# A hybrid retention and HGRN2 trunk on eight cores: two loads moved behind other weights, the sample tile moved to the end, and a new model of the DMA queues in the planner

## The reference: what is computed

```
h = RMSNorm(x) * g_pre
u = h @ W_in                       # 1024 x 4096, eight segments of 512 columns:
                                   # rq rk rv rg hq hf hi hg  (segments 0 to 7)
rq, rk = rotary(rq), rotary(rk)
f  = lb + (1 - lb) * sigmoid(hf);  hk = 1 - f;  hq = silu(hq)
o_r, S_ret  = retention(rq, rk, rv, decay per head)     # recurrent over chunks
o_h, S_hgrn = hgrn2(hq, hk, hi, log f)                  # recurrent over chunks
o  = concat(silu(rg) * head_norm(o_r), silu(hg) * head_norm(o_h))
y  = o @ W_out                                           # 1024 x 1024
out = x + RMSNorm(y) * g_post
```

## Time and profile before

| | us |
|---|---|
| median of 3 executions | 387.5 |
| lowest and highest | 386.18, 388.3 |
| the profiled execution | 388.32 |
| its span on core 7, first to last instruction | 386.8 |
| spans of the eight cores | 381.1 to 386.8 |
| TensorE busy on core 7 | 358.8 (93% of the span) |
| VectorE busy | 255.6 (66%) |
| GpSimd busy | 205.5 (53%) |
| ScalarE busy | 180.9 (47%) |

### The profile page before, as it was taken

How to read it: one execution, slowest core, us unless ns; L and a number is a source line. 1 busy time by engine, 2 the same in 40 slices (tenths; PEclk the granted TensorE clock), 3 DMA queues, 4 the chain that set the end, 5 groups by cost and what they waited for, 6 DMA issues and landing times.

```text
span 386.8 us, 8100 instructions; the slowest of 8 cores (381.1 to 386.8 us)
## 1 busy us (share of the span) xinstructions
PE 358.8 (93%) x2339; PEld 188.1 (49%) x2339; DVE 255.6 (66%) x554; ACT 180.9 (47%) x563; POOL 205.5 (53%) x277
## 2 busy tenths in 40 slices
PE   8599799998988989997999999999999999999982
PEld 8554354455544444453545454545455554554541
DVE  0316565827889998969395949386849467486364
ACT  2431245557767546471636253446262533646341
POOL 8525541545775785774283645375837436347130
PEclk9989899999999999998999999999999999999988
DMA  7999999996488476964537335432233443233217
GB/s 177 204 177 165 202 163 168 178 242 150 87 219 173 157 169 146 231 160 102 153 67 190 88 121 73 164 71 64 55 125 72 133 107 97 110 56 79 101 22 225
DMA packets 64700, 52.62 MB, mean 136 GB/s; under 512 B 45840, under 2 KB 53040, under 8 KB 64656
## 3 DMA queue, kind: packets, MB, share of 16 engines
q1 hardware_dynamic: 59344, 41.61, 42.4%
q0 software_dynamic: 5312, 10.49, 17.7%
HBM read 41.73 MB, written 10.09 MB: 134 GB/s over the span
## 4 chain that ended last, share of the span: by engine, by line
PE 78%; DVE 6%; DMA 5%; issue 3%; POOL 3%; ACT 2%; SPq 1%; DVEq 0%; ACTq 0%; POOLq 0%; another core or an unknown queue 0%
PE bank L671 42%; PE bank L947 14%; PE bank L654 12%; DMA xr<-xp 4%; PE bank L867 2%; PE bank L835 2%; DVE xbf L619 2%; PE bank L872 2%; PE bank L884 2%; POOL QTh L731 1%; DVE fG L713 1%; DVE fR L725 1%; PE bank L934 1%; DMA ogT<-og 1%; SPq L849 1%
## 5 line engine op out<-in xcount | busy, mean ns | idle before, releaser
L671 PE MATMUL bank<-Wi,xT 128*128 128x512 bf16 (+1 forms) x816 | 187.8, 382 | 0.7 <-DVE Sst L889 0.7
L671 PEld LDWEIGHTS bank<-Wi,xT 128*128 128x128 bf16 (+1 forms) x816 | 78.3, 99 | 88.1 <-issue 4.1
L947 PE MATMUL bank<-Wo,ogT 128*128 128x512 bf16 (+1 forms) x272 | 65.1, 391 | 3.6 <-DMA ogT<-og 2.0
L905 DVE SCALAR_TENSOR_TENSOR og<-bank,rsq,gate 128x128 bf16<-128x128 f32 (+1 forms) x136 | 38.6, 343 | 41.2 <-POOL rsq L902 18.3
L654 PE MATMUL bank<-xT,Wi 128*128 128x512 bf16 (+1 forms) x320 | 63.0, 342 | 2.1 <-POOL QTh L731 0.9
L654 PEld LDWEIGHTS bank<-xT,Wi 128*128 128x128 bf16 x320 | 26.9, 98 | 34.2 <-issue 6.9
L947 PEld LDWEIGHTS bank<-Wo,ogT 128*128 128x128 bf16 (+1 forms) x272 | 26.5, 100 | 34.7 <-issue 7.4
L824 POOL TENSOR_TENSOR Sst<-Sst,decS 128x512 f32<-128x512 f32 x30 | 32.9, 1105 | 16.5 <-DVE Sst L889 8.7
L895 ACT ACTIVATE og<-bank 128x128 bf16<-128x128 f32 (+1 forms) x136 | 35.4, 291 | 9.7 <-PE bank L867 6.2
L902 POOL TENSOR_TENSOR rsq<-ssq,mhalf 128x4 f32<-128x4 f32 (+1 forms) x34 | 35.4, 1042 | 5.2 <-POOL ssq L899 0.4
L828 ACT ACTIVATE Sb<-Sst 128x512 bf16<-128x512 f32 x30 | 19.0, 634 | 38.7 <-POOL Sst L824 21.3
(11 more groups left out here) (93 smaller groups left out, 450.8 us busy)
## 6 DMA issues: line engine op xcount, KB each, us to landing
xr<-xp SPq DMA_DIRECT2D x18, 512.0 KB, 4.3
yp<-xr SPq DMA_DIRECT2D x16, 512.0 KB, 2.9
xs<-xp SPq DMA_DIRECT2D x14, 512.0 KB, 5.5
Wi<-w_in POOLq DMA_DIRECT2D x6, 1024.0 KB, 48.5
Wi<-w_in POOLq DMA_DIRECT2D x4, 512.0 KB, 20.3
Wo<-w_out POOLq DMA_DIRECT2D x2, 1024.0 KB, 71.8
rot<-rot_p SPq DMA_DIRECT2D x16, 96.0 KB, 5.0
gpre<-g_pre SPq DMA_DIRECT2D x1, 512.0 KB, 6.7
```

The lines of the kernel that those rows point to most:

```text
L671: ins = e.matmul(pb(v)[0:L, :], lhsT=k.xT[:, kc, j * 128:j * 128 + L], rhs=Wi[:, kc, seg * 512:(seg + 1) * 512], start=(kc == 0), stop=(kc ...
L905: S.op(DVE, lambda e, q_=q_, h=h, vo=vo: e.scalar_tensor_tensor(out=ogs[vs][0:L, h * 128:(h + 1) * 128], in0=pb(vo)[0:L, q_ * 128:(q_ + 1) ...
L947: ins = e.matmul(pb(y)[0:L, :], lhsT=ogT[:, kc, 0:L], rhs=Wo[:, kc, n * 512:(n + 1) * 512], start=(kc == 0), stop=(kc == 7))
```

## The change

There are four edits.

1. The x loads of tiles 0 and 1 of block 1 wait for `("Wi", 5, 3)` instead of `("Wi", 7, 3)`.
2. The load of `gpost` waits for `("Wi", 7, 3)` instead of the first scores.
3. The sample's `front` and `tile` are recorded after tile 3 of block 3 instead of before it (the conditions with `4` in the diff are constants: the first is never true, the second always).
4. The planner's model of DMA is replaced. Before, each queue had its own clock: 275 bytes per ns for large loads of the GpSimd queue from 11.5 us on, 300 for SyncE's queue or 120 while the other is busy, 150 for transposes. Now a class `Net` serves the two queues together, 310 bytes per ns in all (230 before 12 us), with 45% for SyncE's queue while both are busy; transposes have no rate of their own. Every engine starts at 0.9 us in the plan instead of 0. As the plan's times decide the order, the order of the instructions on all engines can differ.

No operation is added to the program or taken from it except that the number of fillers may change. Two parts of the diff are left out here: a test for the cost of a GpSimd operation that the kernel does not use, and a noise on the priorities that is off.

```diff
--- before.py
+++ after.py
@@ -21,20 +21,63 @@
 N_CORES = 8
 
 N_BANKS = 8
-DMA_RATE = 300.0
-SW_RATE = 275.0
-HW_SHARED = 120.0
+DMA_RATE = 310.0
+DMA_RATE_0 = 230.0
+HW_SHARE = 0.45
 
 class Bank:
     def __init__(self, reserve):
         self.reserve = reserve
         self.idx = 0
+
+class Net:
+    def __init__(self):
+        self.t = 0.0
+        self.queues = ([], [])
+        self.coming = []
+
+    def issue(self, t, soft, nbytes, op):
+        self.coming.append([max(t, self.t), 0 if soft else 1, float(nbytes), op])
+        self.coming.sort(key=lambda x: x[0])
+
+    def advance(self, until):
+        out = []
+        while True:
+            while self.coming and self.coming[0][0] <= self.t:
+                c = self.coming.pop(0)
+                self.queues[c[1]].append([c[2], c[3]])
+            on = [q for q in self.queues if q]
+            nxt = self.coming[0][0] if self.coming else None
+            if not on:
+                if nxt is None or (until is not None and nxt > until) or out:
+                    break
+                self.t = nxt
+                continue
+            rate = DMA_RATE if self.t > 12000.0 else DMA_RATE_0
+            rates = [rate] if len(on) == 1 else [rate * (1.0 - HW_SHARE), rate * HW_SHARE]
+            stop = self.t + min(q[0][0] / r for q, r in zip(on, rates))
+            if nxt is not None:
+                stop = min(stop, nxt)
+            if until is not None:
+                stop = min(stop, until)
+            for q, r in zip(on, rates):
+                q[0][0] -= r * (stop - self.t)
+            self.t = stop
+            for q in on:
+                if q[0][0] < 1.0:
+                    out.append((q.pop(0)[1], stop))
+            if until is not None and stop >= until:
+                break
+            if until is None and out:
+                break
+        return out
 
 class Sched:
     def __init__(self):
         self.ops = []
         self.last_w = {}
         self.readers = {}
+        self.jitter = None
 
     def op(self, eng, fn, reads=(), writes=(), dma_key=None, deps=()):
         oid = len(self.ops)
...
@@ -184,9 +231,9 @@
         for i, o in enumerate(ops):
             if ndeps[i] == 0:
                 avail[o["eng"]].append(i)
-        free_t = {e: 0.0 for e in ENGS}
-        sw_free, hw_free, cold = 11500.0, 0.0, 0.0
-        port_free = 0.0
+        free_t = {e: 900.0 for e in ENGS}
+        cold, port_free = 0.0, 0.0
+        net = Net()
         order = {e: [] for e in ENGS}
         done = 0
 
@@ -195,6 +242,19 @@
             if len(fr) <= v.reserve:
                 return None
             return min(fr, key=lambda k: (free_at[k], k))
+
+        def landed(until):
+            out = net.advance(until)
+            for i, t in out:
+                o = ops[i]
+                t += o["lat"]
+                o["t_land"] = t
+                for sx in succ[i]:
+                    ready_t[sx] = max(ready_t[sx], t + XLAT)
+                    ndeps[sx] -= 1
+                    if ndeps[sx] == 0:
+                        avail[ops[sx]["eng"]].append(sx)
+            return len(out)
 
         while done < n:
             best = None
@@ -225,6 +285,8 @@
                         cand = ((st_, -prio[i], i), i, st_)
                 if best is None or cand[2] < best[2] or (cand[2] == best[2] and prio[cand[1]] > prio[best[1]]):
                     best = (e, cand[1], cand[2])
+            if landed(best[2] if best is not None else None):
+                continue
             if best is None:
                 raise RuntimeError("no operation can be placed: held by lines %s, waiting %s" % (
                     [[(ops[u]["line"], "t_start" in ops[u]) for u in users[v]] for v in held],
@@ -256,29 +318,23 @@
             done += 1
             dlat = o["lat"]
             if o["dma_key"] is not None:
-                if e == POOL:
-                    if o["nbytes"] > 600000:
-                        sw_free = max(fin, sw_free) + o["nbytes"] / SW_RATE
-                        dlat = (sw_free - fin) + o["lat"]
-                    else:
-                        dlat = 4500.0
-                else:
-                    share = 9000.0 < fin < sw_free
-                    hw_free = max(fin, hw_free) + o["nbytes"] / (HW_SHARED if share else DMA_RATE if o["lat"] > 1500.0 else 150.0)
-                    dlat = (hw_free - fin) + o["lat"] + (3000.0 if share else 0.0)
-                o["t_land"] = fin + dlat
-                o["t_dma"] = o["nbytes"]
+                net.issue(fin + (4500.0 if e == POOL else 0.0), e == POOL, o["nbytes"], i)
+                if e != POOL and o["nbytes"] < 120000 and len(net.queues[0]) > 1:
+                    o["lat"] += 3500.0
             for v in o["banks"]:
                 left[v] -= 1
                 free_at[v.idx] = max(free_at[v.idx], fin + o["lat"] + (XLAT if e != PE else 0.0))
+            if o["dma_key"] is not None:
+                continue
             for sx in succ[i]:
-                lat = dlat + XLAT if ops[sx]["eng"] != e or o["dma_key"] is not None else (0.0 if e == PE else dlat + 60.0)
+                lat = dlat + XLAT if ops[sx]["eng"] != e else (0.0 if e == PE else dlat + 60.0)
                 if fin + lat > ready_t[sx]:
                     ready_t[sx] = fin + lat
                 ndeps[sx] -= 1
                 if ndeps[sx] == 0:
                     avail[ops[sx]["eng"]].append(sx)
-        self.est_makespan = max(free_t.values())
+        landed(1e9)
+        self.est_makespan = max(max(free_t.values()), max(o.get("t_land", 0.0) for o in ops))
         return order
 
     def add_fillers(self, order, filler):
@@ -603,7 +659,7 @@
                 if i < 4:
                     S.ops[xid]["boost"] = 20e6 - 1e6 * i
                 elif i < 6:
-                    S.ops[xid]["deps"].add(S.last_w[("Wi", 7, 3)])
+                    S.ops[xid]["deps"].add(S.last_w[('Wi', 5, 3)])
             n0 = len(S.ops)
             junk, jk = (xbf[slot], [("xbf", slot)]) if i >= 4 else (gate[i], [("gate", i, 0), ("gate", i, 512)])
             sq = i % 4
@@ -838,7 +894,7 @@
                 if g == 0:
                     sc0[0] = scid
                     for did in late_dma:
-                        S.ops[did]["deps"].add(scid)
+                        S.ops[did]["deps"].add(S.last_w[("Wi", 7, 3)])
                     del late_dma[:]
                 S.op(DVE, lambda e, g=g, vsc=vsc: e.tensor_tensor(out=AT[0:L, g * 4:(g + 1) * 4, 0:L],
                                                                   in0=pb(vsc)[0:L, 0:4 * L].rearrange("p (h t) -> p h t", h=4),
@@ -1032,11 +1088,14 @@
         for b in range(4):
             front(blocks[b])
             if b == 3:
-                for j in range(3):
+                for j in range(4):
+                    if j == 4:
+                        front(smp)
+                        tile(smp, 0)
                     tile(blocks[b], j)
-                front(smp)
-                tile(smp, 0)
-                tile(blocks[b], 3)
+                if 4 == 4:
+                    front(smp)
+                    tile(smp, 0)
             else:
                 for j in range(4):
                     tile(blocks[b], j)
```

More of the change, by code:

```diff
@@ L123, in f @@
                         self.port = name not in ("memset", "affine_select")
-                        if kw.get("op") == ALU.pow:
+                        if kw.get("op") == ALU.pow or kw.get("op1") == ALU.pow:
                             self.cost += 380.0 + 150.0 * n
@@ L175, in list_schedule @@
             prio[i] += o.get("boost", 0.0)
+        if self.jitter is not None:
+            noise = np.random.RandomState(self.jitter[0]).uniform(-1.0, 1.0, n) * self.jitter[1]
+            for i in range(n):
+                prio[i] += float(noise[i])
         XLAT = 110.0
```

## The result

The changed kernel takes 403.6 us in the median of four executions (400.8 to 406.1), against 387.9 for four of the kernel before: a ratio of 1.040, 95% interval 1.032 to 1.049. I had forecast 383.5, in a range of 378 to 391. All eight cores are slower, with spans of 394.0 to 402.6 us against 381.1 to 386.8. Times from here on are medians of the executions in which no die stood in the slower state with a lower granted clock.

The account below looks back on a forecast made before the run. TensorE's work plus its idle and lower-clock time was taken as the bound. Terms -0.6 - 0.2 + 0.5 - 2.7 - 1.5 + 0.5 + 0 = -4.0 us took 388.3 to 384.3, median 383.5; range 378.0 to 391.0.

Parts of the forecast that it names:

- the transpose term of edit 4: Weight stream: two to four block 1 transposes fall into it, each 1.0 us dearer than planned; +0.5 (0 to +5).
- The rival with `Wo`: End of weights: transposes and x tiles delay `Wo` to as late as 102.4, stalling TensorE; +2.6, median 390.1, chance 0.16.
- forecast near 58: Sign on SyncE's queue: the x loads of block 1 should be issued near 58 us.
- forecast before 82: Sign on VectorE: the first `xbf` of block 1 should stand before 82 us.
- The -4.2 us that I put on this: TensorE's idle or slow time returned by earlier block 1 x: -2.7 from 87.4 to 124, -1.5 from 124 to 180 us.
- the lead is swallowed: Rival, 87 to 180 us: x is early, but TensorE's order keeps as many holes; median 387.7, chance 0.20.
- Edit 1's price: Early x loads take 2 x 2.0 us from the fourth weight pair, landing at 73.9 instead of 71.9; +0.5 (0 to +2).
- the 2.0 us forecast: Third weight pair lands 2.0 us earlier, near 57.7, once `gpost` is moved away from ahead of it.
- The 0.6 us that I put ahead of 42.9: Second weight pair: moving `gpost` lets TensorE resume earlier after its pause; -0.6 (0 to -1.0).
- Edit 3: Tail: recording the sample last was to cost nothing; term 0, between -2 and +3.
- the slow last product at 5.30 us: Tail: the product with `Wo`, 16 matmuls after a wait, stays at 5.30 us against 3.5 at full clock.
- The last product with `Wo`: Sign in the tail: it should start some 12.6 us ahead of the end of the span, as before.

Follow-up runs that it names:

- e5: Changed kernel, same TensorE order; block 1's first two DMA transposes replaced by whole-row copies into a scratch, their xT constant: 393.4 us, ratio 1.014.
- e2: Changed kernel, replanned, with xT of block 1's first two tiles transposed by TensorE instead of DMA: 389.6 us, ratio 1.007.
- e8: Changed kernel, replanned, with block 1's first two tiles transposed by TensorE and the sample before tile 3: 389.2 us, ratio 1.003.
- e11: Kernel before, old planner, replanned with block 1's x loads waiting for the third weight pair and its first two tiles transposed by TensorE: 388.8 us, ratio 1.004.
- e6: Kernel before with exactly its order; only the wait of block 1's two x loads moved to the third weight pair after planning: 387.9 us, ratio 1.001.
- e12: Kernel before with only the sample moved after tile 3 of block 3: 388.5 us, ratio 1.003.
- e9: Kernel before with its planner's weight-stream rate at 278 instead of 275: 391.3 us, ratio 1.009.
- e14: Kernel before with its planner's rate for the shared SyncE queue at 125 instead of 120: 392.5 us, ratio 1.012.
- e16: Kernel before with its planner's weight-stream rate at 272 instead of 275: 388.0 us, ratio 1.001.
- e10: Changed kernel; its planner lands a transpose later by what is left of the weight stream, at most 12.5 us: 397.2 us, ratio 1.024.
- e17: Changed kernel; its planner counts transposes at twice their bytes and lands them later by what is left of the weights: 392.8 us, ratio 1.013.
- e13: Kernel before with the new planner model alone, each DMA transpose counted at twice its bytes: 390.5 us, ratio 1.009.
- e7: Kernel before with the new planner model of DMA alone: 395.9 us, ratio 1.021.
- e15: Kernel before with the new planner model alone, its DMA rate at 313 instead of 310 bytes per ns: 398.8 us, ratio 1.030.
- e1: Changed kernel with exactly its order; block 1's first two DMA transposes issued as plain copies of the same bytes: 402.6 us, ratio 1.041.
- e4: Changed kernel with the sample recorded before tile 3 of block 3 again: 401.9 us, ratio 1.039.
- e3: Changed kernel, replanned, with x of block 1 waiting for all of W_in again: 393.0 us, ratio 1.015.

## Why the prediction was wrong

**The step that failed** is the transpose term of edit 4. I wrote: "two to four of these fall into the weight stream, 1.0 us dearer than planned each", +0.5 with bounds of 0 and +5. Two fell into it, and the first was 12.0 us later than planned (84.9 against 72.9), the second 8.5 (87.0 against 78.5). I priced the transpose by the DMA time that it takes from others, 1.9 us, and not by the time that it takes itself beside a full queue. The trace of before had no transpose beside the stream (the first was issued after the weights had all but landed), so the price was not to be read there; but it had transfers of 96 KB that took 8 to 10 us beside it, and these were a sign that latency there isn't size over rate. The bound of +5 came from the wrong quantity too. A slip beside it changed nothing: 2.1 MB read take 6.3 us by the row that I named, not 6.1.

**The place of the stall.** The rival with `Wo` named the right kind of event, a dear transpose beside the weights and TensorE's list stopping in order, and a chance of 0.16 for being slower by it. Its victim was wrong: `Wo` landed at 84.4, earlier than before (90.8). Before, four loads of x went beside it, issued between 71.99 and 73.6. Now one such load stands behind the first transpose, three and `gpost` are issued from 82.36 on, behind the second, and from 73.0 to 84.4 SyncE's queue moved only 0.39 MB beside 1.45 MB of the weights, which at the 0.166 MB per us of the earlier trace rows would have taken 8.7 us alone instead of 11.4. The reader of `xT` itself stopped the list, for 10.9 us, and then 2.7 us went to the lower clock. e5 puts the transfer in many pieces at 10 us of the 16, the late landing and the held queue together, in the same order.

**The lead of x.** x was issued at 56.07 (forecast near 58) and the first norm stood at 68.0 (forecast before 82), so the loads did what was said. The -4.2 us that I put on this didn't come: e2, e8 and e11 use the lead, TensorE waits for no transpose between 60 and 180 us in them, and they stand 0.3 to 0.7% above the kernel before. The rival "the lead is swallowed", 387.7, fits these three, which carry TensorE's 1.2 us of transposes as well. In e2 the idle time was moved ahead and not reduced. In e11 it is less from 60 to 180 us, 7.2 us instead of 8.5 in the mean of the cores, but 1.9 us more stand ahead of 60 us and behind 340.

**Edit 1's price** was right: in e6 the fourth pair lands 4.0 us later in the mean of the cores (71.0 before, 75.0), where I had 4.0 for the two loads alone, and nothing waits for it. In the changed kernel it lands at 73.1 in the mean, where I had 73.9.

**Edit 2** gave the third pair near the 2.0 us forecast. On the two profiled slowest cores 59.7 went to 55.9, but the cores of one execution differ by over 2 us here (57.1 to 59.7 before, 55.9 to 58.1 after), and their means are 58.3 and 56.8. The other runs agree: 56.4 to 57.1 with edit 2, 58.1 to 59.1 without. The 0.6 us that I put ahead of 42.9 didn't come: the second pair lands at 42.4 before and 42.6 after in the mean. No instruction waited for `gpost`. Alone the edit was not tried.

**Edit 3** at 0 was right, in part by luck: 401.9 without it against 403.6, and 388.5 with it against 387.6. I had kept the slow last product at 5.30 us. It now takes 3.61, at full clock, but the sample's chain of waits near 366 us puts sixteen matmuls at 6.19 us where others take 3.6, and e12 shows the same pair, 3.61 and 4.91. The last product with `Wo` starts at 391.74, 10.9 us ahead of the end of the span; I had 12.6.

**Edit 4 as a whole** was costed through two rates and the transpose alone. Its own cost by itself, 8 to 12 us in two draws, is larger than anything in my sum. About 5 us of it go when a transpose counts double. I named no price for a new order as such, and e9 and e14 show that this can be 4 to 5 us in this program for changes that mean nothing (e16: none). My range should have had that on its upper side.

**What stays open.** The second wait, 4.13 us at 169.83, is put down to VectorE's scan; in e5 the same wait (4.28) stands at 161.90, so it belongs to the changed order and not to the late transpose, but it was not taken apart. Why e10 keeps 397 with no long wait is answered only in part by e17. Two draws of a model are few, and e13 is one draw: that the order it gave is some 5 us better is measured, that this is the price and not luck is not shown. Why e7 and e15 are slow is open: in the mean of the cores TensorE idles for 6.4 and 8.5 us more than before and is busy for 2 to 3 us more, spread over many waits.

## What to carry to other kernels

Before a small or many-piece DMA is moved into a stretch in which another queue fills the DMA engines, look up how long transfers of its queue took there from issue to landing, whatever their size, and count pieces; in this program the size over the rate was no guide. A planner's cheapest plan may be cheap where its model is wrong in its favour: here the plan with the earliest end, 374.3, was the slowest on the chip, while that of e2, whose planner gives 374.7, took 389.6. So compare a plan's few decisive landings with a profile before its end is believed. And where a change makes a planner run again, redraw it with a meaningless change of a constant first; only what exceeds that scatter is the change's.

## What the runs showed of the hardware

Beside a full GpSimd queue and from 36 us on, transfers of SyncE's queue in 128 pieces took 7.6 to 12.4 us, from 96 to 512 KB; those above 10.9 had another one right ahead of them, and the last of four loads in a row took 17.3. In the crowded start of the kernel before, the 96 KB of `rot` took 17.9 to 23.2. Transfers of 256 KB in 1,024 or more pieces took 13.2 to 16.5 us when issued between 69 and 77 us, whether transposed (15.4, 13.7; 16.5, 15.1 in e10) or copied (14.9, 13.2). What stood behind such a transfer was late with it: a 512 KB load of x in 128 pieces took 15.2 us behind the first transpose. With the weights gone the same transpose took 3.1 us.

The 15 us are no fixed latency: it was the end of the weights that counted. In the five runs that issue the first such transfer 13 to 16.6 us ahead of the last weights' landing (the changed kernel, e1, e4, e10, e17) it landed 0.2 to 0.6 us behind them, on each of the forty cores. Issued 8 to 11 us ahead (e2, e8) it landed 0.9 to 2.5 us behind them, 5 to 7 us ahead (e3) 1.3 to 4.0, and in no run and on no core before them. The copy of whole rows in e5, issued at 71.1 in the mean of the cores, landed at 78.6, with the last of the weights at 92.7. Why so is not shown.

While 1.45 MB in 739 packets of the weights passed, 1,087 packets with 0.39 MB of SyncE's queue did, so about three small packets for two large ones, and the small ones carried little. The Trainium skill (DMA: Bandwidth & Descriptors, Queues, rings and completion order) says that each DMA engine takes turns between the queues that have work, and drains a whole packet, typically 9 to 17 descriptors, before it switches. The counts agree in kind with taking turns; whether the profile's packets are the page's, and how many descriptors one turn holds, no run here shows.

An instruction that only issues a DMA can hold SyncE for long: the second transpose took 8.86 us to issue, and in e1 the x load behind the two copies 8.03. In e5, with whole rows, the same two issues took 0.47 and 0.52 us.
